# Latent attention in a hybrid encoder: scores and row maxima two steps ahead, and another order of three activations on ScalarE

## The reference, cut to what matters

```python
q = (rms_norm(c_q, q_norm_g) @ w_uq).reshape(b, t, MLA_HEADS, MLA_QK)
kv = (rms_norm(c_kv, kv_norm_g) @ w_ukv).reshape(b, t, MLA_HEADS, MLA_NOPE + MLA_V)
q = apply_partial_rope(rms_norm(q, q_head_g), cos, sin)
k = apply_partial_rope(rms_norm(k, k_head_g), cos, sin)
p = softmax(q k^T * MLA_QK ** -0.5)        # for each head, over all 528 keys
o = p @ v
```

## Time and profile before

| | us |
|---|---|
| median of 3 runs | 2339.93 (2337.79 to 2340.47) |
| profiled execution | 2344.09 |
| its span | 2342.3 |
| PE busy | 2118.8 (90%) |
| PE weight loads busy | 1822.7 (78%) |
| DVE busy | 1089.6 (47%) |
| POOL busy | 997.9 (43%) |
| ACT busy | 854.8 (36%) |

### The profile page before, as it was taken

How to read it: one execution, slowest core, us unless ns; L and a number is a source line. 1 busy time by engine, 2 the same in 40 slices (tenths; PEclk the granted TensorE clock), 3 DMA queues, 4 the chain that set the end, 5 groups by cost and what they waited for, 6 DMA issues and landing times.

```text
span 2342.3 us, 33441 instructions
## 1 busy us (share of the span) xinstructions
PE 2118.8 (90%) x13634; PEld 1822.7 (78%) x13634; DVE 1089.6 (47%) x1699; ACT 854.8 (36%) x1400; POOL 997.9 (43%) x592
## 2 busy tenths in 40 slices
PE   7999998878778999999989999988777779999999
PEld 7888886556667999999988888865555557888887
DVE  8642354555565644441066322545555657444400
ACT  3322343566554222222223222435665543222221
POOL 4365333664312444444433554336642124444444
PEclk9999999899999999999999999998999899999999
DMA  4211111000001222223322211110000012232333
GB/s 155 64 56 62 47 55 54 10 1 19 19 19 46 83 91 90 91 90 99 99 73 64 64 55 55 46 63 10 1 19 19 19 35 92 91 99 91 98 102 114
DMA packets 40040, 143.85 MB, mean 61 GB/s; under 512 B 4433, under 2 KB 4561, under 8 KB 39761
## 3 DMA queue, kind: packets, MB, share of 16 engines
q1 hardware_dynamic: 39888, 141.72, 18.9%
HBM read 139.60 MB, written 2.10 MB: 60 GB/s over the span
## 4 chain that ended last, share of the span: by engine, by line
PE 71%; DVE 14%; ACT 8%; issue 4%; POOL 1%; DMA 1%; ACTq 0%; SPq 0%; DVEq 0%; POOLq 0%
PE pb L800 44%; PE pb L831 6%; PE pb L830 6%; PE pb L832 6%; ACT ebuf L1383 3%; DVE kh L1779 2%; PE pb L1226 2%; DVE rowmax L1825 1%; ACT ebuf L1394 1%; DVE proj L1761 1%; DVE mbuf L1847 1%; ACT rstd L1358 1%; PE pb L1082 1%; ACT rstd L1359 1%; PE pb L930 1%
## 5 line engine op out<-in xcount | busy, mean ns | idle before, releaser
L584 POOL TENSOR_TENSOR parts<-raw,parts 128x1024 fp32r<-128x1024 f32 x248 | 604.8, 2439 | 844.4 <-ACT parts L1434 844.2
L800 PE MATMUL pb<-mix,parts 128*128 128x264 f32 x4608 | 671.0, 294 | 40.3 <-POOL parts L584 17.1
L800 PEld LDWEIGHTS pb<-mix,parts 128*128 128x128 f32 x4608 | 609.5, 194 | 65.6 <-issue 28.1
L1434 ACT ACTIVATE parts<-raw 128x1024 fp32r<-128x1024 f32 x248 | 262.4, 1058 | 826.7 <-PE pb L800 525.1
L800 PE MATMUL pb<-proj_r,parts 128*128 128x264 f32 x3104 | 429.1, 286 | 0.5 <-POOL parts L584 0.5
L800 PEld LDWEIGHTS pb<-proj_r,parts 128*128 128x128 f32 x3104 | 401.2, 189 | 0.8 <-issue 0.7
L830 PE MATMUL pb<-proj_r,parts 128*128 128x512 f32 x528 | 207.4, 393 | 0.8 <-DVE mbuf L1761 0.8
L832 PE MATMUL pb<-proj_r,parts 128*128 128x512 f32 x528 | 207.7, 393 | 0.0
L831 PE MATMUL pb<-proj_r,parts 128*128 128x512 f32 x496 | 198.0, 399 | 0.0
L1767 DVE TENSOR_TENSOR h<-h,pb 128x528 f32<-128x528 f32 (+1 forms) x48 | 33.3, 694 | 272.7 <-PE pb L800 139.1
L1383 ACT ACTIVATE ebuf<-pb,negmax 128x528 f32<-128x528 f32 x160 | 110.9, 696 | 56.0 <-DVE negmax L1826 55.5
(11 more groups left out here) (273 smaller groups left out, 2877.7 us busy)
## 6 DMA issues: line engine op xcount, KB each, us to landing
raw<-w_stream SPq DMA_DIRECT2D x250, 512.0 KB, 3.5
w_head<-w_heads SPq DMA_DIRECT2D x8, 512.0 KB, 4.8
h<-x_t SPq DMA_DIRECT2D x8, 264.0 KB, 6.6
out_t<-h SPq DMA_DIRECT2D x8, 256.0 KB, 4.9
con<-consts SPq DMA_DIRECT2D x1, 1652.5 KB, 10.3
par<-params SPq DMA_DIRECT2D x1, 340.0 KB, 4.4
con<-consts SPq DMA_DIRECT2D x1, 128.0 KB, 6.8
```

What stands on the lines that cost most here:

```text
L584: nc.gpsimd.tensor_tensor(parts[:, n % PARTS, 1, :], w, parts[:, n % PARTS, 0, :].bitcast(FP32), ALU.subtract).then_inc(split.sem, 1)
L800: last = nc.tensor.matmul(pb[rows_, 2 * p + a, 0:HALF], lhs_t, rhs[:, a * HALF:(a + 1) * HALF], start=start, stop=stop)
L1434: nc.scalar.activation(parts[:, n % PARTS, 0, :], raw[:, r % RAW, :], ACT.Copy).then_inc(lead_ready.sem, 1)
```

## The change

PE issues the scores of steps 0 and 1 ahead of the loop, and in step n those of n+2 instead of n+1. DVE does the same with the maxima, and in every step takes the reciprocal of n+1 ahead of the rests of n (before, that was so only for i = 0). ACT takes the exponential of n+1 first in every step, then, for i of 1 to 4, the leads of n, then the scaling of n+1; for i = 0 its order stays. No instruction is added or removed, and no buffer is changed.

```diff
                 pe.wait_ge(v_ready.sem, v_ready.at(l, NT))
                 scores(0)
+                scores(1)
                 for n in range(N_ATT_M):
                     hd, i = n // NT, n % NT
-                    if n + 1 < N_ATT_M:
-                        scores(n + 1)
+                    if n + 2 < N_ATT_M:
+                        scores(n + 2)
...
                 for n in range(N_ATT_M):
                     hd, i = n // NT, n % NT
+                    if n + 1 < N_ATT_M:
+                        softmax(l, n + 1)
                     if i:
                         turned_leads(l, n)
                     if n + 1 < N_ATT_M:
-                        softmax(l, n + 1)
                         scaled_map(l, n + 1)
...
                 row_max(l, 0)
+                row_max(l, 1)
                 inverse_sum(l, 0)
                 for n in range(N_ATT_M):
                     hd, i = n // NT, n % NT
-                    if n + 1 < N_ATT_M:
-                        row_max(l, n + 1)
-                    if i:
-                        turned_rests(l, n)
+                    if n + 2 < N_ATT_M:
+                        row_max(l, n + 2)
                     if n + 1 < N_ATT_M:
                         inverse_sum(l, n + 1)
-                    if i == 0:
-                        if hd >= 1:
-                            half_added(l, hd - 1)
-                        turned_rests(l, n)
+                    if i == 0 and hd >= 1:
+                        half_added(l, hd - 1)
+                    turned_rests(l, n)
                     prepare(prep, n)
```

## The result

The changed kernel takes 2309.45 us (median of 4 runs, 2306.94 to 2310.49) against 2340.20 for the one before (4 runs): ratio 0.9862, 95% interval 0.9845 to 0.988. The sign was right, and so was what the change does in a steady head; the slow copy and the clock were not priced rightly, and with them the size was missed.

A forecast was written before the change was run, and what follows sets the result against it. No engine full; each head a chain through four engines, with PE waiting in three places. Terms sum to 8.85 us a layer, 17.7 for two; 2344.09 less 17.7, less 4.16 to the median: 2322.2; range 2315 to 2330, wider 2311 to 2334.

The forecast's parts named there:

- a: Steady head, from the square of step 1 to Q: Q starts at 3.88 us instead of 4.09, gain 0.21.
- b: Steady head, from the square of step 3 to A: A starts at 3.62 us instead of 4.14, gain 0.52.
- c: Steady head, from A to T(hd+1,1): earlier map, so T at 4.94 us instead of 5.58, gain 0.64.
- The thin cover of a: Before Q: T(3), delayed by later rests, is over at 3.7 us, just before Q could start; minus 0.2 a head in the range.
- a wait takes the place: Rival: T waits for rests wherever it waited for the map; 4.2 us gained, 2336, about no change; chance of no change 0.10.
- slower: Rival: in steps 2 and 4 of heads 0 to 5, turns come 0.80 us later; 2345 to 2355; chance 0.09.
- More than the sum: Rival: PE's three waits in a head all close, 3.26 us a head instead of 1.37; half gives 2313; chance 0.15.
- Start and last steps: Stage start: T(0) 1.1 us later, behind step 2's scores; head 7: T(7,2) to T(7,4) shorter by 0.85 and 1.05.
- The slow copy of the earlier trace lies where it lay, so heads of 22.40 gain the same: Heads with POOL's conversions: DVE's copy stays as slow, so they too gain 1.37 us, to about 21.0.
- the clock paragraph: Step 2's scores at the start (first) may raise the clock sooner, PE's 3.2 us tile wait (second) delay it; sum unchanged.
- Head 6: PE's wait for the weight tile takes back 0.64 us, an earlier map for T(6,4) gives 0.47.
- a rival for the clock: PE falls to 1.2 GHz in one more place a layer, costing 3 us a layer, 2328; no separate chance given.

The follow-up runs named there:

- order_only: The kernel before with only the new order on ACT (exponential first) and DVE (reciprocal ahead of rests), scores and maxima one step ahead: 2352.08 us, 1.0044.
- s2_behind_filled: The changed kernel with step 2's score product behind T(0) and an unused product in PE's wait ahead of T(0): 2317.98 us, 0.9894.
- after_early_tile: The changed kernel with the first weight tile rounded by ACT in step (5,4) and split by POOL ahead of its last rotation: 2304.98 us, 0.9840.
- before_copy_first: The kernel before with DVE's 48x528 copy taken ahead of its wait for K's product: 2328.07 us, 0.9946.
- s2_behind: The changed kernel with the score product of step 2 behind T(0) instead of ahead of it: 2320.42 us, 0.9915.

## Why the prediction was wrong in size

**The steady head was right.** a, b and c came out at 0.34, 0.54 and 0.74 (counted in head 4 against head 5 of before) where 0.21, 0.52 and 0.64 were forecast; 1.5 of these 1.6 arrive in the heads without conversions, 4 and 5, where 1.37 were forecast. All idle times ahead of Q, A and T(hd,1) are within 0.1 of the forecast. The thin cover of a held: no turn but T(hd,1), as before, waited for rests, so neither "a wait takes the place" nor "slower" happened. `order_only` shows the slower rival's mechanism at work where maxima are late. "More than the sum" came nearest in its time (2313) and not in its mechanism: PE's three waits did not close.

**Start and last steps were right.** T(0) is 0.95 later (forecast 1.1), T(7,1) to T(7,4) went from 9.77 to 7.83 (forecast 7.87).

**The step that failed first** is "The slow copy of the earlier trace rows lies where it lay, so heads of 22.40 gain the same". I moved everything in the head and assumed that the copy would meet the same POOL instruction at the same point. Counted from A, the conversions stand where they stood, L610 at 6.44 and L612 at 8.05 in both kernels; the copy came 0.64 earlier, at 7.60 to 7.71 instead of 8.24 to 8.35, and so ahead of L612. Heads 1 to 3 gained 6.8 us in the first layer (T(1,1) to T(4,1) from 67.30 to 60.49) where 4.1 were forecast, and 7.2 in the second: 5.8 us over the forecast, of which 0.13 a head, 0.8, is the surplus that heads 4 and 5 have too. The copy's part is 5 us: 0.76 in five of these heads, and 1.1 in the second layer's head 3.

**The second** is the clock paragraph: "the first would give back at most the 1.1 of the start, and the second falls in a wait that is there already; the sum stands." The first gave 1.3 a layer in T(0,1) to T(0,2), beyond the start, where K lies. At the second the time went the other way: T(6,1) to T(6,2) stayed at 7.9 where 8.5 was forecast, and the two turns behind it took 2.90 each instead of 3.65 and 3.56, since the upper level was back before them. Head 6 gained 1.5 and 1.6 us where it was to lose 0.17. Together the clock made 5.9 us in these two executions. The 2.5 us of head 0 came with the product ahead of T(0), in the changed kernel as in all others that have one there. The 3.4 us of head 6 no run ties to the change: two kernels with the old order had the short low stretch too, and `s2_behind_filled`, with the changed order in head 6, had the long one and the 8.5 that was forecast. So this part of the gain was luck as far as the runs show. I had a rival for the clock, but only in the direction of a slower kernel.

The sum of this: 5.0 for the copy, 5.9 for the clock and 1.6 for the surplus of 0.13 in six heads and two layers are 12.5 of the 12.75 between 2322.2 and 2309.45. Without the 3.4 of head 6 the time would have been about 2313 (an estimate from these sums), inside the wider range (from 2311) and outside the narrower one (from 2315).

**What stays open.** What sets the length of the low stretch at the tile, 3.4 us in one trace and 6.8 in another, is not shown; nor is how often either comes, with one trace of each kernel. `after_early_tile` shows only what is gained where the clock does not fall. Between the stages single executions spent from 48 to 60 us at the lower level, and took 1004.5 to 1009.6 us there in kernels without the moved copy; the hold of `after_early_tile` moves a time by 5 us. So edits worth a few us can't be told by whole times.

## What to carry to other kernels

Putting an exponential ahead of other work on ScalarE paid here only once its maximum was a step old; the steps ahead gave half of the gain alone, and the order alone cost time, so try an order again once its inputs are made earlier. Where a DVE copy and a POOL instruction overlap, a shift of 0.64 us took most of the wait away here, so price such heads from the position of both instructions, or move the copy to where nothing runs. Price the clock with both signs, and see in more than one trace whether a low stretch is the edit's doing: behind the same wait of PE it was 3.4 us long in one and 6.8 in another.

## What the runs showed of the hardware that was not expected

- A copy of 48x528 in fp32 on DVE takes 0.43 us, and 1.30 when it starts 0.3 us behind a POOL instruction; it was held by a TENSOR_TENSOR (1.30) and by the last 0.36 us of a TENSOR_SCALAR (0.64). A copy of 64x12, 0.15 when free, took 2.38 when a POOL instruction of 2.35 started within 0.01 us of it (`after_early_tile`, and `before_copy_first` in code that its edit does not touch). The other eleven traces run the same code in both layers and do not have it.
- The lower level of PE's clock, 1.2 GHz, ended 5.9 us behind T(0) in the kernel before, where PE had idled 1.47 ahead of T(0), 1.4 behind it in the changed kernel, where a product filled most of that wait, and 9.2 behind it in `s2_behind`, where PE idled 1.85 ahead of T(0) and 1.39 ahead of T(0,1).
- Behind PE's wait of 2.6 us for the weight tile the lower level lasted 6.8 us in three stages and 3.4 in five; behind one of 3.25 us 3.4 in eight and 6.8 in two.
- An exponential with its row sum holds ACT for 0.68 us from its start to the start of the next instruction, not for the 0.80 worked out from the earlier trace rows (1.01 to the map, less 0.23 idle).
